# Order of ScalarE, VectorE and SyncE work at three stage changes of a two-layer diffusion trunk

## The chip, the cores and the metric

The kernel runs on one core of a Trainium2 chip. The metric is the device time of one execution in microseconds (us); a comparison uses the median of several executions. Engine names follow the profile: PE is TensorE, PEld its weight loads, ACT is ScalarE, DVE is VectorE, POOL is GpSimd and SP is SyncE, which only issues DMAs.

## The reference, cut to what matters

One inference step of a trunk with two layers, over 128 context tokens and 512 latent tokens of width 1024. Each layer is a mixer and a ConvFFN, each behind an RMS norm with a per-stream scale and shift and a gated residual:

```python
h = rmsnorm(x, P['norm_mix_g'][i]) * (1 + sc1) + sh1
y = mixer(h)                       # layer 0: SSD scan || short convolution; layer 1: attention
x = x + g1 * y
h = rmsnorm(x, P['norm_ffn_g'][i]) * (1 + sc2) + sh2
x = x + g2 * conv_ffn(h, P, i)     # (gelu(dwconv(h @ w_gate)) * (h @ w_up)) @ w_down
```

Layer 1's mixer projects `h` to queries, keys and values (`na_w_qkv`), attends over a neighbourhood plus the context keys, and projects back (`na_w_out`). All of it is float32.

## The kernel before, in words

**Layout.** `x` and the activations lie transposed: 8 chunks of 128 channels on the partitions, 644 token columns each (128 context, 4 padding, 512 latent). A weight slot is a strip of 1024x128 weights; 8 chunks by 128 output channels. PE makes one output tile per slot: for each chunk k, four matmuls with the high part of the weights (against the high and the low part of the activations, in two halves of 322 columns) and two with the low part of the weights, 48 matmuls in all.

**The chain of a weight slot.** SP loads the strip into `raw` (2 buffers, `weights`, L348, issue at L353) once POOL has finished the low part of the slot two before. ACT copies it to `w_hi` rounded (`split`, L1087, the ACTIVATE on L1092; ring of 4, so it waits until PE has used the slot four before). POOL subtracts, `w_lo = raw - w_hi` (`low`, L547, L550). PE waits for that. Each engine runs its own instructions strictly in the order written.

**The chain of an activation chunk at a stage change.** When PE has finished output tile m, DVE adds it to `x` (`residual`, L1821, three instructions on L1827) and frees the PSUM tile. ACT writes the high part of chunk m (`scaled_high`, L1120, two instructions on L1125) and its squares (`square`, L1097, L1103; one buffer, so it waits until the former squares were summed). DVE writes the low part (`deferred_low`, L1546, two casts for the padding on L1551 and two instructions on L1554) and sums the squares into `acc` (`add_squares`, L1477, L1482). The first tile of the next stage waits, chunk by chunk, for the low parts (`whole_tile`, L631). After it PE sums the squares over channels (`norm_stats`, L644, L655), which needs all eight squares; ACT takes the roots (L1109), DVE the reciprocal (L1515), and in the middle of its second tile PE spreads them over the tokens (`norm_spread`, L658). The scale by the norm is applied behind the matmul, so the first tile does not wait for it.

**First stage change, mixer of layer 0 to its ConvFFN.** The last output tile, m = 7, reads the buffers into which the high and low parts of the new stage go, and frees them chunk by chunk (`act_free`). ACT's `out_turn` (L1303) does, for m = 6: the split of weight slot 2 of the ConvFFN, six high parts, the wait for the residual, high part 6, squares 6; for m = 7: the split of slot 3, the wait, high part 7, squares 7. DVE (L1838 to L1850) does residual 6, the sum of squares 6, low parts 0 to 6, residual 7, low part 7, the sum of squares 7.

**Second, ConvFFN of layer 0 to the projections of layer 1.** In the last eight down tiles each tile takes two slots. ACT's `turn` (L1283) splits two slots per tile and, between the second split and the next tile, waits for the residual and does high part and squares. After the last tile SP spills `x` to HBM (L484), waits for it, loads the two context caches (L499, L500) and 16 small bias windows (L493), and only then the weights of the value tiles 4 to 7, then keys and queries. Each value tile is scaled by DVE into `vs` (`take`, L1921), copied into eight windows `vwin` (L1945, L1946), which PE transposes (`v_windows`, L966, L972) and ACT copies to `vtok` (`v_taken`, L1360, L1363). ACT's loop over the eight value tiles does split, then `v_taken`.

**Third, attention output to the ConvFFN of layer 1.** The output projection has eight tiles; ACT does, for each, the split of a slot four ahead, the wait for the residual, squares (L1431 to L1440); for the last tile, behind the split and ahead of the wait, high parts 0 to 6.

Of the kernel before, what the change touches and what calls it, by code (L numbers as in the profile page):

```python
# [23 lines left out]
P = 128  # L24
# [105 lines left out]
def trunk(nc, x_prompt, x_sample, state_ssd, cache_k, cache_v, c, c_ctx, ada_w, ada_b, norm_mix_g, norm_ffn_g,  # L130
# [6 lines left out]
    with ExitStack() as ctx:  # L137
# [209 lines left out]
        def _(sp):  # L347
# [143 lines left out]
            def window_load(hh, windows):  # L491
                for r in range(ROWS):
                    sp.dma_start(win[QW * r:QW * r + QW, hh], windows[r]).then_inc(S[f"win_loaded{hh}"], 16)  # L493

            sp.wait_ge(S["act_ready"], 4 * C)
            sp.wait_ge(S["squares_summed"], 4)
            sp.wait_ge(S["x_spilled"], 32)
            sp.wait_ge(S["table_stored"], 16)
            sp.dma_start(kc[:], cache_k[0, 0].rearrange("s h d -> s (h d)")).then_inc(S["caches_loaded"], 16)  # L499
            sp.dma_start(vc[:], cache_v[0, 0].rearrange("s h d -> s (h d)")).then_inc(S["caches_loaded"], 16)  # L500
            for hh in range(2):
                window_load(hh, windows_of(hh))
            for part in range(3):
                b = SLOT_QKV + part * C
                with sp.Fori(1 if part == 0 else 0, 2) as i:
                    for s in range(4):
                        weights(b, i, s, rows(w_qkv, 0, C, QKV[part] + (4 * i + s) * P))
            for s in range(4):
                weights(SLOT_NA, 0, s, rows(w_no, 0, C, s * P))
            with sp.Fori(0, C - 1) as i:  # L510
# [572 lines left out]
        def _(act):  # L1083
# [197 lines left out]
            def tiles_added(n, b, tb, last_slot, splits):  # L1281

                def turn(i, splits):  # L1283
                    for s in range(4):
                        if splits:
                            split(b + 4, i, s)
                        if s in last_slot:
                            k = last_slot.index(s)
                            act.wait_ge(S[f"tile_free{k}"], tb // 2 + 1 + i)
                            square(n, x, 2 * i + k, first=scaled_high if n == 3 else None)  # L1290
                            if n == 5:
                                act.wait_ge(S["gx_turned"], 2 * i + k + 1)
                                a(gx[:, k], x[:, bass.ds((2 * i + k) * T, T)], ACT.Copy, scale=par[:, bass.ds(R_FIN + k + 2 * i, 1)]
                                  ).then_inc(S["gx_ready"], 1)

                if n == 5:
                    act.sem_inc(S["gx_turned"], 2)
                    act.sem_inc(S["out_copied"], 2)
                with act.Fori(0, C // 2 - 1) as i:
                    turn(i, True)  # L1300
                turn(C // 2 - 1, splits)

            def out_turn(i, pair):  # L1303

                b = SLOT_OUT + 4 + 4 * pair
                for s in range(2):
                    split(b, 2 * i, s)
                if pair == 1:
                    copy_row(5, ADA_STEPS * (C + 1) + ADA_STEPS * i, 2 * C + 2 + 4 * i)
                for k in range(2):  # L1310
                    m = 2 * pair + k + 4 * i
                    split(b, 2 * i, 2 + k)
                    if m == C - 2:
                        act.wait_ge(S["slot_used"], SLOT_OUT + OUT_SLOTS - 2)
                        for c0 in range(C - 2):
                            scaled_high(2, c0)
                    act.wait_ge(S[f"tile_free{k}"], TILE_OUT // 2 + pair + 1 + 2 * i)
                    if m >= C - 2:
                        scaled_high(2, m)
                    square(2, x, m)  # L1320

            for i in range(2):
                for pair in range(2):
# [97 lines left out]
            for part in range(2):  # L1421
                for s in range(4):
                    m = 4 * part + s
                    split(SLOT_NA + 4 * part + 4, 0, s)
                    if m == C - 1:
                        for c0 in range(C - 1):
                            act.wait_ge(S["act_free"], 4 * (C - 1) + c0 + 1)
                            scaled_high(4, c0)
                    act.wait_ge(S[f"tile_free{s % 2}"], (TILE_NA + m) // 2 + 1)
                    if m == C - 1:  # L1430
                        scaled_high(4, m)  # L1431
                    square(4, x, m)
            late_inverse(4)
            ffn(1)
            a(eps[:, 1:2], eps[:, 0:1], ACT.Sqrt)
# [11 lines left out]
        def _(dve):  # L1447
# [386 lines left out]
            for i in range(2):  # L1834

                for pair in range(2):
                    if pair == 1:
                        dve.wait_ge(S["mod_turned"], C + 1 + i)  # L1838
                        modulation((SECS - 2) * C + C * i, ps[:, 4, 0:2 * C])
                    for k in range(2):  # L1840
                        m = 2 * pair + k + 4 * i
                        residual(SLOT_OUT + 4 * pair + 3 + k + 8 * i, k, m, 2, 2 if m < C - 1 else None)
                        if m == C - 2:
                            for c0 in range(C - 1):
                                dve.wait_ge(S["act_free"], 3 * (C - 1) + c0 + 1)
                                deferred_low(2, c0)
            deferred_low(2, C - 1)
            add_squares(2, C - 1)

            def ffn(lay):  # L1850
                b, tb, f = SLOT_FFN[lay], TILE_FFN[lay], lay * FC
# [242 lines left out]
```

## Time and profile before

| what | value |
|---|---|
| median of 3 runs | 2083.84 us (2082.85 to 2084.32) |
| the profiled execution: its own time | 2088.62 us |
| its span, first to last instruction | 2086.8 us |
| granted TensorE clock over the span | 0.973 |
| PE / DVE / ACT / POOL busy, share of the span | 94% / 50% / 33% / 31% |

All durations come from the profiled execution; the 1.8 us between its own time and its span lie outside the instructions. A busy PE is one that has a matmul under way, not one at its peak. A row of a timeline gives the start (us from the span's start), the time to the end of the last of the instructions that it groups, engine, line, operation, what is written from what, the count, and in brackets the idle time of the engine before it and what ended it.

### The profile page before, as it was taken

The page shows a single profiled execution, that of the slowest core. Times are in us where ns is not written, and L with a number is a line of the kernel's source. Part 1 is how long each engine was busy: PE and PEld are TensorE (multiplying, and loading weights), DVE is VectorE, ACT ScalarE, POOL GpSimd, SP SyncE. Part 2 cuts the span into 40 slices and gives each one's busy share as a digit, 9 for nine tenths or more (in the row PEclk, how much of TensorE's full clock was granted, in tenths as well). Part 3 has the DMA queues.
Part 4 walks back from the last instruction along what each step waited for, and adds up shares of the span by engine and source line. Part 5 has one row for each costly group of instructions (what it writes and reads, how often), then busy time and mean ns, then how long its engine had stood idle before and what let it go on. Part 6 is the DMA issues. An engine that isn't in the chain of part 4 may idle for free. (4 is left out here: it accounts for less than half of the span.)

```text
span 2086.8 us, 36378 instructions
## 1 busy us (share of the span) xinstructions
PE 1971.2 (94%) x13563; PEld 1887.0 (90%) x13563; DVE 1042.2 (50%) x1987; ACT 687.4 (33%) x1043; POOL 637.7 (31%) x314
## 2 busy tenths in 40 slices
PE   6699999899999899999999988989999999999997
PEld 3498888787889899999999988989998999999997
DVE  3544776666661365521555334656635655125543
ACT  1433222222231244422323422127724434223333
POOL 0322222222223233344334522332212333433342
PEclk9899999999999999999999999999999999999998
DMA  8123444344444222223222341221031222232222
GB/s 290 41 58 89 145 145 144 120 135 148 129 166 145 81 64 71 70 69 90 71 70 57 97 136 52 71 56 29 19 132 43 80 80 58 75 89 70 65 64 73
DMA packets 280040, 192.31 MB, mean 92 GB/s; under 512 B 25370, under 2 KB 267414, under 8 KB 279462
## 3 DMA queue, kind: packets, MB, share of 16 engines
q1 hardware_dynamic: 276950, 185.61, 29.7%
q10 hardware_dynamic: 3024, 5.78, 0.7%
q8 instruction: 46, 0.75, 0.2%
q14 instruction: 20, 0.16, 0.0%
HBM read 181.31 MB, written 10.06 MB: 92 GB/s over the span
## 5 line engine op out<-in xcount | busy, mean ns | idle before, releaser
L550 POOL TENSOR_TENSOR w_lo<-raw,w_hi 128x1024 fp32r<-128x1024 f32 x244 | 591.7, 2426 | 1344.5 <-ACT w_hi L1092 1344.5
L613 PE MATMUL ps<-act_hi,w_hi 128*128 128x322 f32 x2752 | 850.6, 316 | 13.6 <-DVE act_lo L1554 11.6
L614 PE MATMUL ps<-act_lo,w_hi 128*128 128x322 f32 x2624 | 806.3, 313 | 0.0
L617 PE MATMUL ps<-act_hi,w_lo 128*128 128x322 f32 x2752 | 637.2, 313 | 0.0
L613 PEld LDWEIGHTS ps<-act_hi,w_hi 128*128 128x128 f32 x2752 | 528.2, 192 | 26.4 <-issue 16.4
L614 PEld LDWEIGHTS ps<-act_lo,w_hi 128*128 128x128 f32 x2624 | 501.4, 191 | 0.0
L617 PEld LDWEIGHTS ps<-act_hi,w_lo 128*128 128x128 f32 x2752 | 468.2, 190 | 0.0
L1092 ACT ACTIVATE w_hi<-raw 128x1024 fp32r<-128x1024 f32 x244 | 256.4, 1052 | 452.5 <-PE ps L617 400.0
L613 PE MATMUL ps<-f_hi,w_hi 128*128 128x322 f32 x704 | 214.2, 311 | 0.0
L614 PE MATMUL ps<-f_lo,w_hi 128*128 128x322 f32 x704 | 213.7, 310 | 0.0
L1827 DVE SCALAR_TENSOR_TENSOR x<-ps,mod,x 128x128 f32 (+1 forms) x144 | 54.4, 433 | 262.5 <-PE ps L617 262.0
L617 PE MATMUL ps<-f_hi,w_lo 128*128 128x322 f32 x704 | 161.9, 311 | 0.0
L613 PEld LDWEIGHTS ps<-f_hi,w_hi 128*128 128x128 f32 x704 | 133.5, 190 | 0.0
L614 PEld LDWEIGHTS ps<-f_lo,w_hi 128*128 128x128 f32 x704 | 132.8, 189 | 0.0
L1648 DVE SCALAR_TENSOR_TENSOR ft<-fg,par,ft 128x644 f32<-128x644 f32 x44 | 124.3, 2824 | 6.8 <-DVE ft L1647 6.5
L617 PEld LDWEIGHTS ps<-f_hi,w_lo 128*128 128x128 f32 x704 | 118.0, 188 | 0.0
L1863 DVE TENSOR_TENSOR fg<-ps,spread 128x644 f32<-128x644 f32 x44 | 36.5, 830 | 130.8 <-PE ps L617 122.1
L1339 ACT ACTIVATE fe<-ft,gb 128x130 f32<-128x130 f32 x88 | 44.9, 557 | 127.1 <-DVE ft L1648 127.1
L1482 DVE TENSOR_TENSOR acc<-acc,sq 128x644 f32<-128x644 f32 x48 | 65.6, 1367 | 28.1 <-ACT sq L1103 27.7
L1335 ACT ACTIVATE ft<-fg,par 128x644 f32<-128x644 f32 x44 | 36.7, 834 | 127.4 <-DVE fg L1863 127.3
L1647 DVE SCALAR_TENSOR_TENSOR ft<-fg,par,ft 128x644 f32<-128x644 f32 x44 | 43.3, 984 | 44.1 <-ACT ft L1335 43.6
L1343 ACT ACTIVATE f_hi<-fa 128x644 f32 x44 | 32.7, 743 | 95.1 <-DVE fa L1875 95.1
(294 smaller groups left out, 2173.2 us busy)
## 6 DMA issues: line engine op xcount, KB each, us to landing
ada<-in_ada_w SPq DMA_DIRECT2D x40, 1024.0 KB, 5.3
raw<-in_ssd_w_in SPq DMA_DIRECT2D x44, 512.0 KB, 3.9
raw<-in_ffn_w_gate SPq DMA_DIRECT2D x44, 512.0 KB, 3.8
raw<-in_ffn_w_up SPq DMA_DIRECT2D x44, 512.0 KB, 3.8
raw<-in_ffn_w_down SPq DMA_DIRECT2D x32, 384.0 KB, 3.4
raw<-in_na_w_qkv SPq DMA_DIRECT2D x24, 512.0 KB, 3.7
raw<-in_ffn_w_down SPq DMA_DIRECT2D x32, 320.0 KB, 3.2
first<-in_ada_w SPq DMA_DIRECT2D x8, 1024.0 KB, 12.1
```

Source lines behind the costliest of these rows:

```text
L550: g.tensor_tensor(w_lo[:, s], raw[:, s % RAW], w_hi[:, s], ALU.subtract).then_inc(S["low_split"], 1)
L613: t.matmul(out, hi, chunk_of(src_hi, k0 + k, cols), start=start, stop=False)
L614: t.matmul(out, hi, chunk_of(src_lo, k0 + k, cols), start=False, stop=False)
L617: mm = t.matmul(ps[:, 2 * tset + h, 0:HALF], lo, chunk_of(src_hi, k0 + k, cols), start=False, stop=stop)
L1092: a(w_hi[:, s], raw[:, s % RAW], ACT.Copy).then_inc(S["high_split"], 1)
L1335: a(ft[k][:], fg[k][:, 1:T + 1], ACT.Copy, scale=w1).then_inc(S["ffn_mid"], 1)
L1339: ins = a(fe[k][:, lo:hi], ft[k][:, lo:hi], ACT.Gelu_apprx_tanh, bias=gb[:, k, stream:stream + 1])
L1482: tt(acc[:], acc[:], sq[:], ALU.add).then_inc(S["squares_used"], 1)
L1647: st.then_wait(stt(dst[:], buf[:, 0:T], w[:, bass.ds(w0, 1)], dst[:], ALU.mult, ALU.add))
L1648: return stt(dst[:], buf[:, 2:T + 2], w[:, bass.ds(w2, 1)], dst[:], ALU.mult, ALU.add)
L1827: ins = stt(dst, ps[:, 2 * k + bank, lo:hi], gate, dst, ALU.mult, ALU.add)
L1863: tt(F(fg[k][:, 1:T + 1]), V(0), F(spread[:]), ALU.mult).then_inc(S["tile_free0"], 1)
```

## The change

The splits that stand between a residual and the high parts at the stage changes go behind the squares; at the first change ACT no longer waits with the six high parts for the split of slot 2, and DVE sums squares 6 and 7 after all low parts; SP loads value weights 4 to 7 right after the spill is issued and ahead of the caches, and the two halves of the bias windows among the weights of the keys.

```diff
--- before.py
+++ after.py
@@ -492,19 +492,23 @@
                 for r in range(ROWS):
                     sp.dma_start(win[QW * r:QW * r + QW, hh], windows[r]).then_inc(S[f"win_loaded{hh}"], 16)
 
+            def qkv_weights(part, i):
+                for s in range(4):
+                    weights(SLOT_QKV + part * C, i, s, rows(w_qkv, 0, C, QKV[part] + (4 * i + s) * P))
+
+            qkv_weights(0, 1)
             sp.wait_ge(S["act_ready"], 4 * C)
             sp.wait_ge(S["squares_summed"], 4)
             sp.wait_ge(S["x_spilled"], 32)
             sp.wait_ge(S["table_stored"], 16)
             sp.dma_start(kc[:], cache_k[0, 0].rearrange("s h d -> s (h d)")).then_inc(S["caches_loaded"], 16)
             sp.dma_start(vc[:], cache_v[0, 0].rearrange("s h d -> s (h d)")).then_inc(S["caches_loaded"], 16)
-            for hh in range(2):
-                window_load(hh, windows_of(hh))
-            for part in range(3):
-                b = SLOT_QKV + part * C
-                with sp.Fori(1 if part == 0 else 0, 2) as i:
-                    for s in range(4):
-                        weights(b, i, s, rows(w_qkv, 0, C, QKV[part] + (4 * i + s) * P))
+            qkv_weights(1, 0)
+            window_load(0, windows_of(0))
+            qkv_weights(1, 1)
+            window_load(1, windows_of(1))
+            with sp.Fori(0, 2) as i:
+                qkv_weights(2, i)
             for s in range(4):
                 weights(SLOT_NA, 0, s, rows(w_no, 0, C, s * P))
             with sp.Fori(0, C - 1) as i:
@@ -1282,12 +1286,14 @@
 
                 def turn(i, splits):
                     for s in range(4):
-                        if splits:
+                        if splits and not (n == 3 and s in last_slot):
                             split(b + 4, i, s)
                         if s in last_slot:
                             k = last_slot.index(s)
                             act.wait_ge(S[f"tile_free{k}"], tb // 2 + 1 + i)
                             square(n, x, 2 * i + k, first=scaled_high if n == 3 else None)
+                            if splits and n == 3:
+                                split(b + 4, i, s)
                             if n == 5:
                                 act.wait_ge(S["gx_turned"], 2 * i + k + 1)
                                 a(gx[:, k], x[:, bass.ds((2 * i + k) * T, T)], ACT.Copy, scale=par[:, bass.ds(R_FIN + k + 2 * i, 1)]
@@ -1309,15 +1315,19 @@
                     copy_row(5, ADA_STEPS * (C + 1) + ADA_STEPS * i, 2 * C + 2 + 4 * i)
                 for k in range(2):
                     m = 2 * pair + k + 4 * i
-                    split(b, 2 * i, 2 + k)
+                    late = m >= C - 2
                     if m == C - 2:
                         act.wait_ge(S["slot_used"], SLOT_OUT + OUT_SLOTS - 2)
                         for c0 in range(C - 2):
                             scaled_high(2, c0)
+                    if not late:
+                        split(b, 2 * i, 2 + k)
                     act.wait_ge(S[f"tile_free{k}"], TILE_OUT // 2 + pair + 1 + 2 * i)
-                    if m >= C - 2:
+                    if late:
                         scaled_high(2, m)
                     square(2, x, m)
+                    if late:
+                        split(b, 2 * i, 2 + k)
 
             for i in range(2):
                 for pair in range(2):
@@ -1421,8 +1431,9 @@
             for part in range(2):
                 for s in range(4):
                     m = 4 * part + s
-                    split(SLOT_NA + 4 * part + 4, 0, s)
-                    if m == C - 1:
+                    if m < C - 1:
+                        split(SLOT_NA + 4 * part + 4, 0, s)
+                    else:
                         for c0 in range(C - 1):
                             act.wait_ge(S["act_free"], 4 * (C - 1) + c0 + 1)
                             scaled_high(4, c0)
@@ -1430,6 +1441,8 @@
                     if m == C - 1:
                         scaled_high(4, m)
                     square(4, x, m)
+                    if m == C - 1:
+                        split(SLOT_NA + 4 * part + 4, 0, s)
             late_inverse(4)
             ffn(1)
             a(eps[:, 1:2], eps[:, 0:1], ACT.Sqrt)
@@ -1839,13 +1852,14 @@
                         modulation((SECS - 2) * C + C * i, ps[:, 4, 0:2 * C])
                     for k in range(2):
                         m = 2 * pair + k + 4 * i
-                        residual(SLOT_OUT + 4 * pair + 3 + k + 8 * i, k, m, 2, 2 if m < C - 1 else None)
+                        residual(SLOT_OUT + 4 * pair + 3 + k + 8 * i, k, m, 2, 2 if m < C - 2 else None)
                         if m == C - 2:
                             for c0 in range(C - 1):
                                 dve.wait_ge(S["act_free"], 3 * (C - 1) + c0 + 1)
                                 deferred_low(2, c0)
             deferred_low(2, C - 1)
-            add_squares(2, C - 1)
+            for m in (C - 2, C - 1):
+                add_squares(2, m)
 
             def ffn(lay):
                 b, tb, f = SLOT_FFN[lay], TILE_FFN[lay], lay * FC
```

## Rows read from the trace of the kernel before

**Rows 1.** Parts 1 and 5 of the page: busy time by engine; one costly group.

```profile
PE 1971.2 (94%) x13563; PEld 1887.0 (90%) x13563; DVE 1042.2 (50%) x1987; ACT 687.4 (33%) x1043; POOL 637.7 (31%) x314
...
L550 POOL TENSOR_TENSOR w_lo<-raw,w_hi 128x1024 fp32r<-128x1024 f32 x244 | 591.7, 2426 | 1344.5 <-ACT w_hi L1092 1344.5
```

**Rows 2.** Waits of PE, whole span: engine, line, releaser, us in total, times, longest.

```profile
PE ps L684 <- DMA ada<-in_ada_w: 14.9, 8, 2.4
...
PE ps L613 <- DVE act_lo L1554: 11.6, 4, 5.2
PE ps L972 <- DVE vwin L1946: 10.7, 3, 4.7
```

**Rows 3.** Busy time by stretch: length, each engine's busy time (count), granted clock, DMA share, GB/s.

```profile
714.34:719.50 5.16, 0.00 (x0) 0.01 (x1) 4.11 (x8) 1.97 (x3) 2.44 (x1) 0.73 0.01 2
...
760.00:1190.00 430.00, 430.00 (x2896) 430.00 (x2895) 190.76 (x251) 146.49 (x182) 169.32 (x71) 1.00 0.25 73
```

**Rows 4.** Timeline of ACT at the first stage change.

```profile
700.69 0.58 ACT L1164 ACTIVATE arow<-ps 128x512 f32<-128x512 f32 x1
...
708.29 6.44 ACT L1125 ACTIVATE act_hi<-x,scale_a 128x128 fp32r<-128x128 f32 x14
```

**Rows 5.** Timeline of DVE at the first stage change.

```profile
707.27 1.13 DVE L1827 SCALAR_TENSOR_TENSOR x<-ps,mod,x 128x128 f32<-128x128 f32 x3 [3.48 <-PE ps L617]
715.39 0.83 DVE L1482 TENSOR_TENSOR acc<-acc,sq 128x644 f32<-128x644 f32 x1 [6.99 <-ACT sq L1103]
...
716.28 3.09 DVE L1554 SCALAR_TENSOR_TENSOR act_lo<-x,scale_a,act_hi 128x128 fp32r<-128x128 f32 x2
...
725.70 1.12 DVE L1827 SCALAR_TENSOR_TENSOR x<-ps,mod,x 128x128 f32<-128x128 f32 x3
```

**Rows 6.** Timeline of PE at the first stage change.

```profile
729.12 0.41 PE L613 MATMUL ps<-act_hi,w_hi 128*128 128x322 f32 x1 [1.32 <-DVE act_lo L1554]
...
730.11 1.17 PE L655 MATMUL ps<-ones,acc 128*128 128x2 f32 x10
```

**Rows 7.** Timeline of DVE at the third stage change.

```profile
1581.40 2.34 DVE L1482 TENSOR_TENSOR acc<-acc,sq 128x644 f32<-128x644 f32 x1 [0.81 <-ACT sq L1103]
1588.64 1.51 DVE L1551 CAST act_hi<-pads 128x4 fp32r<-128x4 f32 x1 [4.91 <-ACT act_hi L1125]
...
1597.47 1.12 DVE L1827 SCALAR_TENSOR_TENSOR x<-ps,mod,x 128x128 f32<-128x128 f32 x3
```

**Rows 8.** Timeline of PE at the third stage change.

```profile
1600.89 0.42 PE L613 MATMUL ps<-act_hi,w_hi 128*128 128x322 f32 x1 [0.41 <-DVE act_lo L1554]
```

**Rows 9.** Timeline of ACT in the last down tiles of layer 0.

```profile
1188.76 1.02 ACT L1125 ACTIVATE act_hi<-x,scale_a 128x128 fp32r<-128x128 f32 x2 [0.29 <-DVE x L1827]
```

**Rows 10.** Timeline of SP after the spill of x: start, us, what it issues.

```profile
1205.44 0.35 SPq L499 DMA_DIRECT2D kc<-in_cache_k  x1
...
1206.53 7.83 SPq L493 DMA_DIRECT2D win<-bias_table  x16
```

**Rows 11.** Timeline of ACT in the value tiles.

```profile
1209.14 0.60 ACT L1118 ACTIVATE spread<-ps 128x512 f32<-128x512 f32 x1 [0.61 <-PE ps L665]
1218.43 1.06 ACT L1092 ACTIVATE w_hi<-raw 128x1024 fp32r<-128x1024 f32 x1 [8.69 <-DMA raw<-in_na_w_qkv]
```

**Rows 12.** Timeline of DVE in the value tiles.

```profile
1211.18 1.15 DVE L1945 TENSOR_SCALAR vwin<-vs,wb 128x896 f32<-128x896 f32 x1
...
1212.71 0.16 DVE L1923 COPY wb<-ps 128x2 f32<-128x2 f32 x1 [0.19 <-PE ps L617]
...
1233.52 2.35 DVE L1946 TENSOR_SCALAR vwin<-vs,wb 128x128 f32<-128x128 f32 x1
```

**Rows 13.** Timeline of PE in the value tiles.

```profile
1222.10 1.09 PE L972 MATMUL ps<-ident,vwin 128*128 128x128 f32 x8 [1.29 <-DVE vwin L1946]
```

**Rows 14.** Busy time by stretch after two pauses of PE in the first mixer.

```profile
326.08:335.00 8.92, 8.92 (x95) 7.62 (x96) 1.81 (x4) 0.60 (x1) 0.00 (x0) 0.81 0.57 176
374.28:384.00 9.72, 9.72 (x112) 8.42 (x113) 2.41 (x5) 1.34 (x2) 0.00 (x0) 1.00 0.57 175
```


## The prediction, made before the changed kernel ran

> **What bounds the kernel now.** I first read the page. PE has a matmul under way for 1971.2 of 2086.8 us and every other engine for half of the span or less [rows 1], so time can be had only where PE stands still or runs slowly. The waits of PE come next: two entries touch what is changed. The first matmuls of a tile wait for low parts on DVE four times, 11.6 us, and the transposes of the value windows wait for DVE three times, 10.7 us [rows 2]. The stretches place the first entry: at the first stage change PE does nothing from 714.34 to 719.50, and the clock granted there is 0.73, where a long busy stretch has 1.00 [rows 3]. The timelines then show the chain. At the first change ACT has its last free moment at 701.3, behind the copy of a row, and starts the high parts only at 708.29 [rows 4], because the split ahead of them waits for PE; DVE is done with residual 6 at 708.4, but waits 6.99 us for squares 6 before it makes a low part, and residual 7 waits in line until 725.70 [rows 5]. PE resumes at 719.52, waits again for chunk 7 until 729.12 and sums squares from 730.11 [rows 6]. At the third change the same pattern holds: DVE idles 4.91 us for the first high part and reaches residual 7 at 1597.47 [rows 7], PE has chunk 7 at 1600.89 [rows 8].
>
> One more thing decides much: POOL's subtraction takes 2.43 us [rows 1], and a DVE instruction that reads and writes SBUF and falls into it stands until it ends: a cast of four columns took 1.51 us [rows 7], a window copy of 128 columns 2.35 us [rows 12], a low part of two instructions 3.09 us [rows 5].
>
> **First change.** ACT: with the split moved behind, the six high parts start at 701.3; seven take 6.44 us [rows 4], so six are done by 706.8. DVE ends residual 6 at 708.40 and goes straight to low parts; PE frees the buffers chunk by chunk ahead of it. A chunk costs 1.07 us (from the cast's end at 1590.15 to 1597.47, less 0.9 for the rest of its own chunk, over six chunks [rows 7]). Chunks 0 to 2 run to 711.6. ACT meanwhile does high part 6, 0.92 us, and squares, 0.63, and then the moved split, 1.1; POOL's subtraction so starts at about 711.1, behind DVE's running instruction, and holds DVE until 711.64 + 2.43 = 714.1. The rest of chunk 3 and chunks 4 to 6 need 0.9 + 3 x 1.07, so residual 7 starts at 718.2, 7.5 us before its 725.70. Chunk 7 is then ready for PE at 729.12 - 7.5 = 721.6. PE's own pace: 2896 matmuls in 430 us [rows 3], 0.148 us each, a tile of 48 in 7.1 us; it starts the tile at 714.25 and reaches chunk 7 at 720.5, so a pause of about 1.1 us remains. What is late next is the sum of squares, now behind all low parts: sum 6, squares 7 (one buffer) and sum 7 in series, 0.83 + 0.72 + 0.83, from 721.6: PE sums at 723.9 instead of 730.11, after a second pause of 1.2. **Gain 6.2 us.** Bounds: 8.5 us if POOL holds nobody (then PE's own pace ends the tile at 721.4), 3.8 us if it holds DVE for another 2.43.
>
> The moved split of slot 3 runs behind squares 7, to 724.1, and POOL's subtraction to 726.6. Queued behind are DVE's small sums and the reciprocal, done at 726.9; PE wants it in the middle of its second tile, at 728.7. Cost nothing while those 1.8 us cover it. The slot itself is wanted two tiles later.
>
> **Third change.** ACT is free at 1581.3 after squares 6, and high part c needs only PE's release of chunk c, every 0.89 us; so they run from 1581.3 to 1587.8, ahead of DVE. DVE ends the sum of squares 6 at 1583.74 [rows 7] and makes seven low parts at 1.07, no subtraction of POOL among them: residual 7 at 1591.2 instead of 1597.47, and chunk 7 at 1594.6 instead of 1600.89 [rows 8]. PE starts the tile without a pause at 1586.4, wants chunk 7 at 1592.7 and pauses 1.9 us. The sum of squares follows low part 7 as now. **Gain 6.3 us**; bounds 8.2 (no pause at all) and 3.9 (one subtraction of 2.43 in the way). Slot 3's split falls on the table load ahead of the roots; 0.4 us are left.
>
> **Down tiles of layer 0.** The odd split moves behind the squares, some 3 us later. High parts now wait 0.29 us for DVE's x and not for the split [rows 9], so nothing is gained; PE uses the slot three slots, 13 us, later, and no wait of PE at this change is in [rows 2] (the four waits there are 5.18, 1.32, 4.73 and 0.41, all at the other two changes). Price 0; without that cover 3 us a tile.
>
> **Value tiles.** SP's order now has two cache loads and sixteen window loads, 7.83 us of issuing [rows 10], ahead of the value loads; slot 4's load lands for the split at 1218.43, for which ACT idles 8.69 us [rows 11], `vtok` and the second windows come late, and PE waits 1.29 [rows 13]. With the load behind the spill (landed by 1205.4 [rows 10]) the split follows ACT's copy of the norm at 1209.65. That removes the 1.29. But POOL's subtraction then starts 1.14 later, at 1210.8, and the first window copy, which starts at 1211.18 [rows 12], falls into it: it ends at 1213.2 + 1.2 = 1214.4 instead of 1212.52. PE has finished the tile at 1212.7 [rows 12], so it pauses 1.75 us. The other two waits, 4.71 each, come from the same collision further on (1233.52 [rows 12]) and stay, since there ACT does copy, split and DVE the window in the same order as now. **Loss 0.5 us**; bounds: gain 1.3 (no collision), loss 3.9 (rival 3). The caches are wanted after eight value tiles, 57 us on; the window loads, 3.9 us per half, stand where SP now waits for slots 7 us apart. Both cost nothing; without the cover, their 7.83 us of issuing.
>
> **The clock.** Four pauses of 1.1 to 1.9 us remain, in three places. In the first mixer PE pauses eight times for `ada`, 14.9 us in all, at most 2.4 [rows 2]. After five the granted clock stays at 1.00, as from 374.28; after three it falls for a while, as from 326.08, where 0.81 over 8.92 us costs 1.7 us [rows 14]. At three in eight for each place one fall is likeliest (0.44; none 0.24, two 0.26): **1.7 us**. The Trainium skill, TensorE: Matmul & The Clock Gate, section "HAM oscillation — how this bites in real kernels", holds that only idle gaps longer than any of these bring the clock down; by it no fall would come and the sum would be 12.0. The trace disagrees for three pauses in eight.
>
> **Sum.** 6.2 + 6.3 - 0.5 - 1.7 = 10.3 us. The profiled execution took 2088.62 us, so it would take 2078.3. The median of the runs shown, 2083.84, is 4.8 us shorter and is what I forecast against: **2073.5 us**.
>
> **Rivals.**
> 1. No fall of the clock: 12.0 us, 2071.8. For it: the pauses are mostly shorter than the 2.4 us one. Against: a pause of 1.91 had a fall behind it. Chance 0.19. It is what that page's section gives.
> 2. POOL's subtractions miss DVE: a start 0.4 us later in the value tiles, or a gap taken at the first change. 8.5 + 6.3 + 1.3 = 16.1 us, 2067.7. Against: 2.43 us is a wide target. Chance 0.12.
> 3. The value loads share the DMA engines with the spill, and the spill, on which DVE's first value tile waits, lands late: a load takes 4.0 us (issued at 1214.4, split at 1218.4 [rows 10, 11]), so two would push it from 1205.4 to 1213.4, where DVE wants it at 1210.0 behind ACT's copy: 3.4 us more, 2076.9. Against: the spill is issued first. Chance 0.10.
> 4. Slower: the two late subtractions of slot 3 end so late that the reciprocal becomes the bound in the middle of the second tile. Each us beyond the 1.8 to 2.2 of cover costs 2, one per ConvFFN: at 7.1 us of lateness the gain is gone, at 9.3 it is slower by 0.2%, at 10 the time is 2089.5. For it: the split, the subtraction and the reciprocal are now one chain behind the last square. Against: it needs a load that is not there in time, and both are there before the split today. Chance 0.10, half of it past the first point only.
> 5. Two or three falls of the clock: 2075.2 or 2076.9. Chance 0.07.
>
> **How the numbers follow.** The forecast keeps 0.42. From rival 2 (2067.7) to rivals 3 and 5 (2076.9) the cases hold 0.90, and by the bounds of the terms some of each lies outside, so the range is 2067.5 to 2077.0. A measurement of this kernel tells about 0.2%, 4.2 us, from no change: all cases but rival 4 are faster by more, 0.90; rival 4 is split into 0.05 for no difference and 0.05 for slower.
>
> **What would show it.** Right: the low parts of the first change begin at 708.4 and PE has no pause at 714; a pause of about 1 us before chunk 7 and another before the sum of squares; at the third change a single pause of about 1.9; a window copy of over 3 us at 1211 and no wait for a value load on ACT. Wrong: PE waiting at the reciprocals, the first value tile of DVE waiting for the spill, or the clock low for longer than in the kernel before after either change.

## The result and the profile after

Four executions of the changed kernel took 2067.24 to 2069.14 us, median 2068.72; the kernel before, run beside it, 2084.08 (2082.85 to 2085.19). The ratio is 0.9925 with a 95% interval of [0.9908, 0.9942]: 15.4 us less, 10.3 were forecast, and 2068.72 lies in the range 2067.5 to 2077.0. Run again later, unaltered (the second run below), the changed kernel took 2075.58 against 2086.18, ratio 0.9938 [0.9914, 0.9962], 10.6 us less. The intervals of the two ratios overlap; what differs between the two is told below.

The profiled execution took 2067.24 us (span 2065.5). Part 1 of its page, to be held against [rows 1]:

```profile
PE 1957.0 (95%) x13563; PEld 1874.6 (91%) x13563; DVE 1043.8 (51%) x1987; ACT 686.2 (33%) x1043; POOL 638.4 (31%) x314
```

Every engine works as much as before, and PE is busy 14.2 us less, although it makes the same 13563 matmuls: it runs less time at the lower clock. The waits of PE over the span, against [rows 2]:

```profile
PE ps L976 <- DVE vwin L1960: 10.0, 3, 4.7
...
PE ps L617 <- DVE act_lo L1567: 2.6, 2, 1.8
...
PE ps L659 <- DVE acc L1495: 1.2, 1, 1.2
```

The waits for low parts went from 11.6 us to 2.6, a new wait for the sum of squares takes 1.2, and the waits for windows lost only 0.7. To see where the time went, both traces (and that of the second run) are cut at marks that all have: the first matmul of PE's sums of squares, the start of residual 6 on DVE, and the first transpose of `kc`.

| stretch | before | changed | changed, second run |
|---|---|---|---|
| start to the sums inside the first mixer, ahead of its output tiles | 583.74 | 575.45 | 586.27 |
| from there to residual 6 | 123.53 | 123.51 | 123.52 |
| residual 6 to PE's sums (first change) | 22.84 | 16.52 | 16.53 |
| ConvFFN 0, down tiles with the second change | 473.07 | 473.18 | 476.12 |
| value tiles, to the transposes of `kc` | 74.43 | 73.56 | 73.80 |
| keys to PE's sums (holds the third change) | 324.28 | 317.92 | 318.23 |
| from there to the last instruction of an engine | 478.79 | 479.25 | 479.17 |

Rows three to six hold the edits: 894.62 us before, 881.18 and 884.68 changed, a gain of 13.4 and of 9.9. The first row holds no edit, yet its work takes 575 us in one execution and 586 in another. Busy time by stretch shows why. Columns: stretch, length, busy time of each engine (instructions), granted clock, DMA share, GB/s. First the kernel before, its first row and 20 us around the first change:

```profile
0.00:583.74 583.74, 514.08 (x3681) 445.32 (x3682) 349.89 (x778) 171.36 (x243) 130.91 (x70) 0.95 0.43 132
...
715.00:735.00 20.00, 14.16 (x85) 13.93 (x86) 14.47 (x42) 3.32 (x7) 2.44 (x1) 0.83 0.09 27
```

The same two of the changed kernel's profiled execution, then of its second run (there from 726):

```profile
0.00:575.45 575.45, 504.42 (x3682) 437.04 (x3682) 350.52 (x778) 171.30 (x243) 130.85 (x70) 0.97 0.43 133
...
715.00:735.00 20.00, 19.52 (x136) 19.52 (x137) 9.67 (x16) 8.81 (x13) 5.20 (x3) 1.00 0.19 54
```

```profile
0.00:586.27 586.27, 515.91 (x3681) 446.94 (x3682) 349.53 (x778) 171.26 (x243) 130.92 (x70) 0.95 0.43 131
726.00:746.00 20.00, 19.68 (x117) 19.68 (x118) 7.75 (x14) 6.96 (x11) 4.75 (x2) 0.83 0.18 52
```

A granted clock of 0.95 over 584 us says that 5% of full-speed time, some 29 us, was lost at the lower level (1.2 of 2.4 GHz); 0.97 over 575 is some 17. The unrounded clock records give 29.0, 18.8 and 30.7 us for the three executions. That is about the difference of the first row: the falls in the mixer come and go between executions, and no edit stands there. Behind the first change the rows read 0.83 before (3.4 us lost in 20), 1.00 in one execution of the changed kernel and 0.83 in the other. In the kernel before that fall is covered by a wait (shown in the part on the prediction); in the second run nothing covers it: the 2.9 us more that it took in ConvFFN 0, most of the 3.5 by which the two gains differ, are one fall of the clock.

**First change.** The timeline of all engines but PE's weight loads, changed kernel, against [rows 4 to 6]:

```profile
698.96 1.13 DVE L1840 SCALAR_TENSOR_TENSOR x<-ps,mod,x 128x128 f32<-128x128 f32 x3 [3.48 <-PE ps L621]
...
701.68 1.05 ACT L1096 ACTIVATE w_hi<-raw 128x1024 fp32r<-128x1024 f32 x1
...
702.81 2.73 POOL L554 TENSOR_TENSOR w_lo<-raw,w_hi 128x1024 fp32r<-128x1024 f32 x1 [7.24 <-ACT w_hi L1096]
...
703.21 2.36 DVE L1564 CAST act_hi<-pads 128x4 fp32r<-128x4 f32 x1
...
709.69 1.11 DVE L1840 SCALAR_TENSOR_TENSOR x<-ps,mod,x 128x128 f32<-128x128 f32 x3
...
713.11 0.41 PE L617 MATMUL ps<-act_hi,w_hi 128*128 128x322 f32 x1 [0.83 <-DVE act_lo L1567]
...
715.48 0.27 PE L659 MATMUL ps<-ones,acc 128*128 128x2 f32 x1 [1.22 <-DVE acc L1495]
...
717.23 0.22 DVE L1528 RECIPROCAL roots<-roots 128x10 f32<-128x10 f32 x1
```

DVE goes from residual 6 straight to the low parts and is at residual 7 after 10.73 us instead of 18.43. The split of slot 2 now comes at 701.68, POOL's subtraction holds a four-column cast for 2.36 us, and PE pauses 0.83 ahead of chunk 7 and 1.22 ahead of the sums: the long pause of 5.18 is gone.

**Third change**, against [rows 7, 8]:

```profile
1565.85 6.46 ACT L1129 ACTIVATE act_hi<-x,scale_a 128x128 fp32r<-128x128 f32 x14
...
1575.72 1.12 DVE L1840 SCALAR_TENSOR_TENSOR x<-ps,mod,x 128x128 f32<-128x128 f32 x3
...
1579.14 0.41 PE L617 MATMUL ps<-act_hi,w_hi 128*128 128x322 f32 x1 [1.75 <-DVE act_lo L1567]
...
1579.95 2.25 DVE L1867 SCALAR_TENSOR_TENSOR wsum<-wsum,par 128x22 f32<-128x22 f32 x1
...
1582.25 0.22 DVE L1528 RECIPROCAL roots<-roots 128x10 f32<-128x10 f32 x1
```

High parts run right behind squares 6, residual 7 comes at 1575.72, and one pause of 1.75 us is left. The subtraction of slot 3 holds DVE's small sum for 2.25, the reciprocal follows at 1582.25, and PE does not wait for it.

**Value tiles**, against [rows 11 to 13]:

```profile
1195.12 1.05 ACT L1096 ACTIVATE w_hi<-raw 128x1024 fp32r<-128x1024 f32 x1
...
1196.25 2.38 POOL L554 TENSOR_TENSOR w_lo<-raw,w_hi 128x1024 fp32r<-128x1024 f32 x1 [7.88 <-ACT w_hi L1096]
...
1196.66 1.15 DVE L1959 TENSOR_SCALAR vwin<-vs,wb 128x896 f32<-128x896 f32 x1
...
1197.72 0.99 DVE L1960 TENSOR_SCALAR vwin<-vs,wb 128x128 f32<-128x128 f32 x1
...
1198.77 1.09 PE L976 MATMUL ps<-ident,vwin 128*128 128x128 f32 x8 [0.62 <-DVE vwin L1960]
```

The wait for the value load is gone, and the subtraction (1196.25 to 1198.63) does start ahead of the first window copy. But that copy, 896 columns, takes 1.15 us as ever and lies wholly inside; only the copy of 128 columns behind it is held, to 1198.71, and PE pauses 0.62.

### The profile page after: what moved, and what is told of

Read it like the earlier page. It is cut to its first block and busy times, and to the rows that moved or that the text cites. A ratio compares the mean times of both kernels' runs of the same rounds, so it can differ in the third digit from the quotient of the medians.

```text
span 2065.5 us, 36346 instructions
## 1 busy us (share of the span) xinstructions
PE 1957.0 (95%) x13563; PEld 1874.6 (91%) x13563; DVE 1043.8 (51%) x1987; ACT 686.2 (33%) x1043; POOL 638.4 (31%) x314
```

## The experiments

### One half of the first change at a time

VectorE's half alone, on the kernel before:

```diff
-   residual(..., m, 2, 2 if m < C - 1 else None)
+   residual(..., m, 2, 2 if m < C - 2 else None)
...
-            add_squares(2, C - 1)
+            for m in (C - 2, C - 1):
+                add_squares(2, m)
```

> The kernel before with VectorE's half of the first change alone (sum of squares 6 behind the low parts); ScalarE still splits slot 2 ahead of the high parts. Measured from the start of residual 6 on VectorE to TensorE's sum of squares: 22.84 us in the kernel before, 16.52 in the changed one. Theory: either half alone breaks the chain, since in the kernel before ScalarE begins the high parts just as residual 6 ends; low parts then follow the high parts one by one, the first held by the subtraction of slot 2, residual 7 some 11 us after residual 6, the stretch 16.7, and the whole run 6 us shorter. Rival 1: the two halves add up, each giving 2 to 4 us: the stretch 19 to 21. Rival 2: ScalarE's half is what counts, and this alone gives under 1 us: the stretch 22 or more.

2081.31 against 2084.36, ratio 0.9985 [0.9972, 0.9997]: 3.0 us less, where 6 were expected. The timeline of DVE and PE, and the clock behind:

```profile
701.02 1.50 DVE L1551 CAST act_hi<-pads 128x4 fp32r<-128x4 f32 x1 [0.99 <-ACT act_hi L1125]
...
707.86 3.14 DVE L1554 SCALAR_TENSOR_TENSOR act_lo<-x,scale_a,act_hi 128x128 fp32r<-128x128 f32 x2
...
711.99 1.12 DVE L1827 SCALAR_TENSOR_TENSOR x<-ps,mod,x 128x128 f32<-128x128 f32 x3
...
715.40 0.41 PE L613 MATMUL ps<-act_hi,w_hi 128*128 128x322 f32 x1 [2.13 <-DVE act_lo L1554]
```

```profile
717.00:737.00 20.00, 19.22 (x113) 19.22 (x114) 7.64 (x12) 6.52 (x9) 2.40 (x1) 0.83 0.06 17
```

Two subtractions hold DVE here (a cast of 1.50 us, a low part of 3.14), squares 7 wait for sum 6, and the stretch is 18.89 us: longer than the theory's 16.7, and just short of rival 1's 19. Whether the halves add up is left to the other half. PE pauses 2.13 us ahead of chunk 7 and 1.2 ahead of the sums, and the clock falls behind: ConvFFN 0 takes 476.27 instead of 473.07. Of the 3.95 us gained in the stretch 0.75 are left behind ConvFFN 0.

ScalarE's half alone:

```diff
+                    late = m >= C - 2
...
-                    split(b, 2 * i, 2 + k)
+                    if not late:
+                        split(b, 2 * i, 2 + k)
...
                     square(2, x, m)
+                    if late:
+                        split(b, 2 * i, 2 + k)
```

> The kernel before with ScalarE's half of the first change alone (the last two splits behind high parts and squares); VectorE still adds squares 6 ahead of the low parts. Theory: squares 6 are now there 1.6 us after residual 6 instead of 7, so VectorE waits 1.6 us and sums for 0.8, and the subtraction of slot 2 then holds one low part by about 2.1: the stretch from residual 6 to the sum of squares is 17.4 us (22.84 before), the whole run 5.4 us shorter. Rival 1 (halves add up): the stretch 19 to 21. Rival 2 (VectorE's order is what counts): 22 or more.

2080.17, ratio 0.998 [0.9962, 0.9998]. The stretch is 17.63 us, as the theory had it, and ConvFFN 0 takes 474.59:

```profile
706.04 3.15 DVE L1558 SCALAR_TENSOR_TENSOR act_lo<-x,scale_a,act_hi 128x128 fp32r<-128x128 f32 x2
...
715.52 1.12 DVE L1831 SCALAR_TENSOR_TENSOR x<-ps,mod,x 128x128 f32<-128x128 f32 x3
...
718.94 0.41 PE L613 MATMUL ps<-act_hi,w_hi 128*128 128x322 f32 x1 [2.13 <-DVE act_lo L1558]
```

Either half brings residual 7 forward by the same 5.2 to 5.3 us (13.10 and 13.22 behind residual 6, 18.43 before); both together by 7.7. In the stretch the halves gain 3.95 and 5.21 us, both together 6.32: the halves don't add up, since each alone breaks the chain, and rival 1 falls. The second half takes PE's longest pause at this change from 2.13 to 1.22 us. Whether that spares falls of the clock is not shown: both variants have one, of 3.4 and of 1.7 us, but so has the second run of the changed kernel. Over the stretch and ConvFFN 0 the gains are 0.75 and 3.69 for the halves, and for both 6.2 in the one execution and 3.3 in the other.

### The third and the second change alone

```diff
-                    split(SLOT_NA + 4 * part + 4, 0, s)
-                    if m == C - 1:
+                    if m < C - 1:
+                        split(SLOT_NA + 4 * part + 4, 0, s)
+                    else:
...
                     square(4, x, m)
+                    if m == C - 1:
+                        split(SLOT_NA + 4 * part + 4, 0, s)
```

> The kernel before with the third change alone (ScalarE's high parts ahead of the split in the output tiles of the attention). Theory: from the transposes of the cache to TensorE's sum of squares before the second ConvFFN 324.3 us become 317.9, as in the changed kernel, and nothing else moves: 6.4 us less in all, with the granted clock at 1.00 behind the pause. Rival: the gain leans on the other changes (slots or loads that they bring earlier), then under 5 us here. Rival: a fall of the clock behind the remaining pause of 1.8 takes 1.7 us back.

2079.39, ratio 0.9974 [0.9961, 0.9987], 5.0 us. The stretch from `kc` to the sums is 318.10 us, 6.2 less, and all stretches ahead of it that hold edits are within 0.02 of the kernel before. DVE comes to residual 7 11.7 us behind residual 6, 18.0 before: the 6.2 us are its chain. No fall of the clock follows the pause of 1.7 us that is left.

```diff
-                        if splits:
+                        if splits and not (n == 3 and s in last_slot):
                             split(b + 4, i, s)
...
+                            if splits and n == 3:
+                                split(b + 4, i, s)
```

> The kernel before with the second change alone, the odd splits of the first ConvFFN's last down tiles behind the squares. Theory: nothing waits for those slots, 13 us are left: the stretch from the first ConvFFN's sums to the next ones stays at 473.06 us within 0.2, and the run at the time of the kernel before. Rival: a high part or a slot comes late once the splits move, up to 3 us a tile, 12 us in all.

2087.73 against 2086.18, ratio 0.9998 [0.9984, 1.0012]; ConvFFN 0 takes 473.08 us, and PE is busy for all of it:

```profile
729.24:1202.32 473.08, 473.08 (x3191) 473.08 (x3190) 209.33 (x280) 163.13 (x205) 182.73 (x76) 1.00 0.26 75
```

### SyncE's order alone

```diff
+            qkv_weights(0, 1)
             sp.wait_ge(S["act_ready"], 4 * C)
...
+            qkv_weights(1, 0)
+            window_load(0, windows_of(0))
+            qkv_weights(1, 1)
+            window_load(1, windows_of(1))
```

> The kernel before with SyncE's order alone. Theory: no wait for a value load is left on ScalarE; the first window copy of 896 columns takes 1.15 us though the subtraction begins ahead of it, only the copy of 128 columns is held, and TensorE pauses about 0.6 us before the first windows and no longer before the second: the stretch from the sums of the first ConvFFN's statistics to the transposes of the cache loses 0.8 us (547.5 before), the two pauses of 4.71 stay. Rival, as predicted: the 896-column copy is held to the end of the subtraction, over 3 us, TensorE pauses 1.75, and the stretch grows by 0.5. Rival: the spill lands so late that VectorE's first value tile waits for it: 3 us longer.

2080.18, ratio 0.9976 [0.9958, 0.9995]; the executions spread over 12 us, so the stretch decides: 73.80 us instead of 74.43, 0.6 less.

```profile
1206.03 1.15 DVE L1949 TENSOR_SCALAR vwin<-vs,wb 128x896 f32<-128x896 f32 x1
...
1207.09 0.99 DVE L1950 TENSOR_SCALAR vwin<-vs,wb 128x128 f32<-128x128 f32 x1
...
1208.14 0.33 PE L976 MATMUL ps<-ident,vwin 128*128 128x128 f32 x1 [0.61 <-DVE vwin L1950]
```

The same picture as in the changed kernel: 1.15 us unheld, 0.99 held, a pause of 0.61.

### What the window copies cost

On the changed kernel, the copy of 128 columns first:

```diff
-   ts(vwin[:, 0:7 * P]..., windows, wb[:, k, 1:2], None, ALU.add)
-   ts(vwin[:, 7 * P:8 * P], vs[:, NLAT:TQ], wb[:, k, 0:1], None, ALU.add).then_inc(...)
+   ts(vwin[:, 7 * P:8 * P], vs[:, NLAT:TQ], wb[:, k, 0:1], None, ALU.add)
+   ts(vwin[:, 0:7 * P]..., windows, wb[:, k, 1:2], None, ALU.add).then_inc(...)
```

> The changed kernel with the two window copies of the value tiles swapped, the one of 128 columns first. Theory: only the 128-column copy is held by a subtraction; ahead of it, it takes 0.28 us in six of the eight tiles, and the 896-column copy still takes 1.15 us though the whole of it may lie inside the subtraction. Windows are ready 2.05 us earlier, the two pauses of 4.71 become 2.65, and the stretch from the sums of squares ahead of the value tiles to the transposes of the cache falls from 73.56 to 69.5 us, or a little less if less half clock follows. Rival: any copy is held that runs in a subtraction; then the 896-column copy takes over 3 us, the pauses stay at 4.7 or grow to 5.8.

2068.89, which as a whole is not to be told from the changed kernel. The stretch is 68.25 us, 5.3 less. The second tile's copies (subtraction from 1207.65), and the waits of PE:

```profile
1206.66 0.29 DVE L1959 TENSOR_SCALAR vwin<-vs,wb 128x128 f32<-128x128 f32 x1 [1.26 <-ACT vtok L1373]
...
1206.86 1.15 DVE L1960 TENSOR_SCALAR vwin<-vs,wb 128x896 f32<-128x896 f32 x1
...
1207.65 2.40 POOL L554 TENSOR_TENSOR w_lo<-raw,w_hi 128x1024 fp32r<-128x1024 f32 x1 [4.53 <-ACT w_hi L1096]
```

```profile
PE ps L976 <- DVE vwin L1960: 6.9, 3, 2.6
```

0.29 and 1.15: the rival that any copy is held falls. The three waits are 6.9 us instead of 10.0 (the first grew to 1.66, where the short copy is held ahead of the long one); the other 2.2 us are clock, 0.99 over this stretch and 0.95 in the changed kernel. The expectation had allowed for a little of that, not for 2.2.

On the changed kernel, the fourth tile's windows transposed one tile later:

```diff
-            v_windows(0, 3)
             for s in range(4):
                 whole_tile(SLOT_QKV, 1, s, TILE_QKV, 4, s)
-                if s > 0:
-                    v_windows(1, s - 1)
+                v_windows(*((1, s - 1) if s > 0 else (0, 3)))
```

> The changed kernel with TensorE's transposes of the fourth value tile's windows put behind the fifth tile instead of ahead of it. Theory: the first pause of 4.71 us is there only because the windows are wanted at once; it goes whole, and with it the 1.7 us that the clock at half cost behind it, since no pause, no fall: the stretch to the transposes of the cache falls from 73.56 to 67.2 us. Rival: the fall comes all the same (the transposes bring it, not the pause): 68.9. Rival: the wait only moves, because VectorE or ScalarE is late one tile on: 72 or more.

The stretch is 67.28 us, as the theory had it: the first pause of 4.71 is gone and nothing took its place. The median of the whole, 2068.66, does not show these 6 us against the changed kernel's 2068.72; why is not shown. The profiled execution, 2074.95, lost 29 us in the mixer and had a fall behind the first change, which the stretch does not contain.

### What is left at the first change

On the changed kernel, sum 6 put into DVE's wait for high part 7:

```diff
+            add_squares(2, C - 2)
             deferred_low(2, C - 1)
-            for m in (C - 2, C - 1):
-                add_squares(2, m)
+            add_squares(2, C - 1)
```

> The changed kernel with the sum of squares 6 at the first stage change put ahead of low part 7, where VectorE waits about 0.9 us for high part 7. Theory: what is late there is the series sum 6, squares 7, sum 7 behind the low parts; with sum 6 in the gap the second pause of TensorE, 1.22 us, goes to 0.2 or less, and the stretch from residual 6 to the sums falls from 16.52 to 15.3. Rival: low part 7 comes later by the 0.83 of the sum, the pause ahead of chunk 7 grows from 0.83 to 1.7 and the stretch stays within 0.3 of 16.5.

```profile
713.88 0.82 DVE L1495 TENSOR_TENSOR acc<-acc,sq 128x644 f32<-128x644 f32 x1
...
716.25 0.41 PE L617 MATMUL ps<-act_hi,w_hi 128*128 128x322 f32 x1 [0.83 <-DVE act_lo L1567]
...
717.25 0.39 PE L659 MATMUL ps<-ones,acc 128*128 128x2 f32 x3
```

The stretch is 15.15 us; the pause ahead of the sums is gone, the one ahead of chunk 7 stays at 0.83, so the sum cost the low part nothing. The whole, 2070.01, does not show 1.4 us.

The changed kernel once more, unaltered (its row stands in the table above):

> The changed kernel, unaltered, once more, for the clock. Theory: the pauses are the same to 0.1 us (0.83, 1.22 and 1.75 at the first and third change), and whether the clock falls behind them differs from execution to execution, since it came after the same pauses in two of the variants and not in two others: about an even chance of 1.7 to 3.4 us lost behind the first change here, and a time of 2069 to 2072. Rival: the changed kernel has none, and the falls of the variants were theirs: nothing lost.

The pauses are the same to 0.02 us, and this time the clock falls behind the first change, by 3.4 us, and not behind the third. So far the theory holds, and the rival falls. The time does not fit: 2069 to 2072 was expected, 2075.58 was the median. The profiled execution, the slowest of four with 2081.51, has 10.8 us more in the first row than the one shown first.

### A version that beats both

On the changed kernel: the swap of the copies, the later windows, sum 6 in the gap, and the last windows and `kc` among the key tiles:

```diff
-            v_windows(1, 3)
...
+                whole_tile(SLOT_QKV + C, 0, s, TILE_QKV + C, 4, s)
+                if s == 0:
+                    v_windows(1, 3)
+                if s == 1:
+                    ...
```

(behind `if s == 1` stand the two waits and the eight transposes of `kc`.)

> The changed kernel with the swap of the copies, the sum in the gap, the fourth tile's windows behind the fifth, and also the eighth tile's windows behind the first key tile and the transposes of the cache behind the second. Theory: both pauses of 4.71, the wait of 1.4 before the cache's transposes and the 4.0 us that the clock at half costs in that stretch go, and 1.2 at the first change: 16 us less than the changed kernel, about 2053. Rival: the falls of the clock stay or come elsewhere: 12 us less, 2057. Rival: the key tiles wait for splits that stand behind the late copies on ScalarE: less than 8 us gained.

2056.46 against 2087.29, ratio 0.9844 [0.9818, 0.9871]; the changed kernel's two ratios were 0.9925 and 0.9938.

```profile
PE ps L976 <- DVE vwin L1962: 1.7, 1, 1.7
```

```profile
720.00:740.00 20.00, 20.00 (x131) 20.00 (x131) 10.05 (x14) 7.33 (x11) 4.81 (x2) 0.91 0.18 53
1568.00:1588.00 20.00, 18.89 (x122) 18.90 (x123) 11.05 (x18) 9.44 (x13) 4.98 (x2) 0.91 0.17 49
```

One wait of 1.7 is left in the value tiles. From the sums ahead of them to the sums behind the third change it takes 375.06 us, the changed kernel 391.48, so the 16 us are there. The whole was expected at 2053 and came nearer to the rival's 2057: there is still a fall behind either change (0.91 over 20 us; 1.7 us by the clock records), here with a single pause of 0.83 and of 1.8.

With the split of slot 2 moved behind squares 7 too:

```diff
-                    if late:
-                        split(b, 2 * i, 2 + k)
+                    if m == C - 1:
+                        split(b, 2 * i, 2)
+                        split(b, 2 * i, 3)
```

> The variant with all four edits, and in it the split of slot 2 at the first stage change moved behind squares 7 as well, ahead of that of slot 3. Theory: the subtraction of slot 2 no longer falls on a low part (2.37 us there), residual 7 comes 2.2 us earlier and the pause before chunk 7, 0.83, goes: the stretch from residual 6 to the sums falls from 15.14 to 14.3. The two subtractions then run in series ahead of the reciprocal; its cover was 2.8 us in the changed kernel, so up to 1 us may come back as a pause at the spreading. Rival (as rival 4 of the prediction): the reciprocal is late by the whole 2.4 and more, and TensorE pauses 2 us or more in the second tile: no gain or a loss. Rival: the loads behind slot 2 come late and a split in the ConvFFN waits for them.

2055.75, ratio 0.9849 [0.9827, 0.987]: not to be told from the variant without it.

```profile
713.68 4.95 POOL L554 TENSOR_TENSOR w_lo<-raw,w_hi 128x1024 fp32r<-128x1024 f32 x2 [15.86 <-ACT w_hi L1098]
...
714.08 2.25 DVE L1870 SCALAR_TENSOR_TENSOR wsum<-wsum,par 128x22 f32<-128x22 f32 x1
...
717.01 0.22 DVE L1531 RECIPROCAL roots<-roots 128x10 f32<-128x10 f32 x1
```

```profile
715.00:735.00 20.00, 20.00 (x142) 20.00 (x141) 10.54 (x14) 8.21 (x11) 6.67 (x4) 1.00 0.27 81
```

The stretch is 14.05 us, PE has no pause left at this change, and the clock stays at 1.00. Two subtractions run in series from 713.68; the first holds a small sum for 2.25, but the reciprocal runs inside the second in its usual 0.22, and PE does not wait. So rival 4's chain has its place but not its price.

## Why the prediction was right, and where it was not

**First change, 6.2 forecast.** The stretch gained 6.32, with the steps as they stood: the low parts start at once, a subtraction holds a cast (2.36 us), residual 7 comes 7.7 us earlier (7.5 forecast), two pauses of 0.83 and 1.22 (1.1 and 1.2 forecast). The subtraction starts 3.85 us behind the start of residual 6, where 3.8 were forecast.

**Third change, 6.3 forecast.** 6.36, with one pause of 1.75 (1.9 forecast). **Down tiles, 0 forecast**: 0.

**Value tiles, a loss of 0.5 forecast.** It was a gain of 0.9 (0.6 in the three other profiles with this order and the copies as they were). The step that failed is "the first window copy, which starts at 1211.18, falls into it: it ends at 1213.2 + 1.2". I had put the hold that [rows 12] show for the copy of 128 columns on the one of 896. Behind it stands a rule made too wide: "a DVE instruction that reads and writes SBUF and falls into it stands until it ends" was drawn from casts, the short copy and low parts. The trace of the kernel before had the counterexample, in the second value tile:

```profile
1219.57 4.72 POOL L550 TENSOR_TENSOR w_lo<-raw,w_hi 128x1024 fp32r<-128x1024 f32 x2 [19.70 <-ACT w_hi L1092]
```

```profile
1220.50 1.15 DVE L1945 TENSOR_SCALAR vwin<-vs,wb 128x896 f32<-128x896 f32 x1 [6.77 <-ACT vtok L1363]
```

The long copy starts 0.93 us into the first of these two subtractions and takes the same 1.15 us as at 1211.18, where none runs. The variants' runs show the same. The Trainium skill, SBUF — State Buffer, section "Who interferes with whom", says that a DVE instruction with one SBUF input contends with GpSimd only in a mode that uses two ports; VectorE: DVE Perf Modes, section "Mode 2×_2P — use both read ports for one tensor", wants the outermost dimensions of source and destination even, or equal, and the long copy reads seven windows and writes one run. The trace agrees with the first: 1.15 us inside the subtraction for the one copy, up to 2.41 for the other. That the seven is the reason, and not the length, was not tried.

**The clock, one fall of 1.7 forecast.** In the profiled execution there was none, as rival 1 had it; in the second run one of 3.4. Four profiles have the changed order and the same two pauses at the first change (the changed kernel twice, the variants with the swap and with the later windows): 0, 1.7, 3.4 and 3.4 us were lost behind them. Eight have the pause of 1.7 to 1.8 at the third change: six lost nothing, two 1.7 and 3.4. The third place, the first windows, came to a pause of 0.62 and no fall. The means of the first two, 2.1 and 0.6, add up to 2.8 where 1.7 stood; the step that failed is "at three in eight for each place one fall is likeliest", since the places differ and a fall can cost 3.4. With so few profiles the means are rough. The Trainium skill, TensorE: Matmul & The Clock Gate, section "HAM oscillation — how this bites in real kernels", gives no fall for such pauses; these runs show falls behind some of them.

**The falls of the kernel before.** It has a fall of 3.4 us behind its long pause at either change, as has every profile with that pause. One could take them for a part of the gain: at the first change PE's pauses shrank by only 4.45 of the 6.32 us, and the rest is matmuls that now run at full clock. But a slow PE cost nothing there. Busy time in the kernel before, from DVE's first low part to its residual 7 at the first change, of PE's work at the lower clock in it, and from the first cast to residual 7 at the third change (columns as above):

```profile
716.28:725.70 9.42, 6.18 (x30) 6.21 (x30) 9.42 (x28) 0.03 (x1) 2.44 (x1) 0.64 0.19 56
719.52:723.53 4.01, 4.01 (x15) 4.01 (x16) 4.01 (x15) 0.00 (x0) 0.00 (x0) 0.50 0.44 131
1588.64:1597.47 8.83, 6.18 (x23) 6.21 (x24) 8.83 (x28) 5.41 (x12) 1.49 (x1) 0.61 0.21 59
```

DVE is busy all the way (9.42 of 9.42 and 8.83 of 8.83 us), and PE, slow as it was, still waited 1.32 and 0.41 us for chunk 7 [rows 6, 8]. At full clock it would have waited longer. So the gain is DVE's chain, as the prediction had it. A fall in the changed kernel that reaches past the sums, as in the second run, has no such cover, and it was right to price it as new.

**Rivals 2 to 4.** POOL did hold DVE at the first change (2). The spill of x ahead of the value tiles takes longer now, 8.9 us from issue to landing instead of 7.6, but DVE's first value tile does not wait for it (3). The reciprocal was not late in any profile, not even behind two subtractions (4).

**The whole.** 13.4 us in the profiled execution and 9.9 in the second run against 10.3. That 9.9 lies so near is in part luck: the value tiles gained 0.6 where a loss of 0.5 stood, and the fall cost 3.05 us in ConvFFN 0 (476.12 against 473.07) where 1.7 stood. The two medians fell by 15.4 and 10.6 us. Medians cannot be cut into stretches, so what the 15.4 hold beyond the edit is not shown. The start of the first mixer, which the edit does not touch, could hold it: it differed by 10.8 us between the two profiles of the changed kernel.

## What to carry to other kernels

Where two engines wait on each other in a circle, reordering either one breaks it, so the gains of the two halves must not be added; price the pair. A pause of the matrix engine costs its length and, in some executions, a fall of the clock behind it; the fall costs time only where no later wait covers it, so ask what the engine waits for next. And read single stretches between marks: here identical work ahead of the edit differed by 11 us between executions, as much as the whole effect.

## What was not expected of the hardware

- A subtraction on POOL holds one DVE instruction and lets another of the same kind pass: a copy of 128 columns took 2.41 us instead of 0.28; one of 896 columns, read as seven windows, took 1.15 us inside it and outside.
- Behind the same pauses of 0.83 and 1.22 us the clock lost 0, 1.7 and 3.4 us in different executions, and in the two variants with a pause of 0.83 alone 0 and 1.7; with no pause at the place it stayed at 1.00, in one profile.
- The reciprocal and the memset ahead of it, on DVE, ran inside a subtraction in 0.22 and 0.06 us, while a small sum of two inputs was held 2.25.
